# Expert loop of a two-layer backbone: a third staging set for chunks 4, 7 and 10, and loads in the order of the casts

## What is computed

```python
def hier_moe(h, lp):
    lg = (h @ lp['moe_w_group'] + lp['moe_b_group']).astype(jnp.float32)
    ...                                        # top-1 of 4 groups, then top-2 of 4 experts in it
    dense_w = jnp.sum(jax.nn.one_hot(eid, N_EXPERTS, dtype=jnp.float32) * tw[..., None], axis=-2)
    hid = jnp.einsum('bsd,edf->bsef', h, lp['moe_w1'])
    gate, up = jnp.split(hid, 2, axis=-1)
    act = jax.nn.silu(gate) * up * dense_w[..., None].astype(h.dtype)
    return jnp.einsum('bsef,efd->bsd', act, lp['moe_w2'])
```

## Time and profile before

| | us |
|---|---|
| median of 3 runs | 1817.4 (1815.0 to 1821.8) |
| the profiled execution's own time | 1818.3 |
| its span, first to last instruction | 1816.2 |
| PE busy in the span | 1649.1 |
| DVE busy | 1171.0 |
| ACT busy | 891.5 |
| expert loop, first layer | 712.7 to about 893 |
| expert loop, second layer | about 1596 to 1774 |

### The profile page before, as it was taken

The page is one execution under the profiler, slowest core; times in us unless marked ns, Lnnn a source line. Parts: engine busy times, 40 slices in busy tenths (PEclk is TensorE's granted clock), DMA queues, the critical chain, the costliest instruction groups (busy, mean ns, idle before and its releaser), DMA issues.

```text
span 1816.2 us, 34273 instructions
## 1 busy us (share of the span) xinstructions
PE 1649.1 (91%) x13317; PEld 1112.9 (61%) x13317; DVE 1171.0 (64%) x1877; ACT 891.5 (49%) x1477; POOL 491.3 (27%) x434
## 2 busy tenths in 40 slices
PE   5899989999989996988889999899999999799886
PEld 3478766777765555444466886667776655554444
DVE  4495355777636757888556926477774394788874
ACT  3322555666642232777543236466664312358763
POOL 0222253221231311233143315322113321123313
PEclk8999999999999998999979999999999999889998
DMA  9565535532335645999935542232223366489975
GB/s 318 185 210 176 170 133 186 195 112 73 100 122 211 208 142 211 339 378 401 323 146 167 195 160 93 80 103 73 77 77 106 125 235 233 151 299 338 402 291 197
DMA packets 191615, 351.33 MB, mean 193 GB/s; under 512 B 15795, under 2 KB 99314, under 8 KB 191218
## 3 DMA queue, kind: packets, MB, share of 16 engines
q1 hardware_dynamic: 182005, 320.17, 50.2%
q0 software_dynamic: 7776, 28.32, 4.2%
q10 hardware_dynamic: 1693, 0.89, 0.2%
HBM read 288.32 MB, written 61.01 MB: 192 GB/s over the span
## 4 chain that ended last, share of the span: by engine, by line
PE 65%; DVE 11%; DMA 9%; ACT 7%; issue 5%; DVEq 2%; SPq 1%; POOL 1%; ACTq 0%; POOLq 0%
PE PS L444 38%; PE PS L451 11%; PE PS L1179 3%; DMA wf<-in_moe_w 3%; PE PS L1163 3%; DMA arena<-in_moe_w 3%; PE PS L949 2%; DVE arena L2560 2%; PE PS L914 1%; ACT whi L1760 1%; PE PS L931 1%; ACT arena L1591 1%; DMA hpart<-y_rows,wulo 1%; DVE wlo L2560 1%; DVE scratch L2500 1%
## 5 line engine op out<-in xcount | busy, mean ns | idle before, releaser
L1883 POOL TENSOR_TENSOR wlo<-wf,whi 128x256 f16<-128x256 f32 (+1 forms) x276 | 294.8, 1101 | 851.2 <-ACT whi L1507 799.3
L444 PE MATMUL PS<-hpart,whi 128*128 128x320 f16 x2048 | 423.4, 300 | 19.0 <-ACT arena L1591 17.8
L444 PE MATMUL PS<-hpart,wlo 128*128 128x320 f16 x1024 | 306.6, 299 | 0.0
L444 PE MATMUL PS<-whi,hpart 128*128 128x256 f16 (+2 forms) x1536 | 287.8, 288 | 9.9 <-issue 6.3
L444 PEld LDWEIGHTS PS<-hpart,whi 128*128 128x128 f16 x2048 | 190.1, 98 | 108.7 <-issue 39.7
L444 PE MATMUL PS<-wlo,hpart 128*128 128x256 f16 (+2 forms) x768 | 219.5, 288 | 0.0
L444 PEld LDWEIGHTS PS<-whi,hpart 128*128 128x128 f16 x1536 | 148.7, 98 | 66.9 <-issue 29.6
L2366 DVE TENSOR_REDUCE stat<-PS 128x1 f32<-128x640 f32 (+1 forms) x160 | 110.7, 713 | 80.0 <-PE PS L1163 77.5
L451 PE MATMUL PS<-hpart,whi 128*128 128x128 f16 (+1 forms) x768 | 138.8, 304 | 12.4 <-DVE hpart L2041 10.8
L1591 ACT ACTIVATE arena<-PS,pcol 128x320 f32<-128x320 f32 x128 | 67.4, 527 | 168.2 <-PE PS L444 163.1
L2194 DVE SCALAR_TENSOR_TENSOR scratch<-scratch,cw 128x655 f32<-128x655 f32 x120 | 138.6, 1197 | 4.5
(11 more groups left out here) (366 smaller groups left out, 2909.2 us busy)
## 6 DMA issues: line engine op xcount, KB each, us to landing
arena<-in_moe_w SPq DMA_DIRECT2D x68, 1024.0 KB, 8.9
arena<-in_w_ada SPq DMA_DIRECT2D x48, 1024.0 KB, 7.1
wf<-in_w_gate SPq DMA_DIRECT2D x32, 1024.0 KB, 5.7
wf<-in_moe_w SPq DMA_DIRECT2D x32, 1024.0 KB, 8.9
g_rows<-arena SPq DMA_DIRECT2D x128, 160.0 KB, 1.8
wf<-in_w_in SPq DMA_DIRECT2D x18, 1024.0 KB, 9.4
y_rows<-scratch SPq DMA_DIRECT2D x34, 512.0 KB, 8.7
arena<-g_rows SPq DMA_DIRECT2D x24, 640.0 KB, 5.2
```

What stands on the lines that cost most here:

```text
L444: ins = pe.matmul(out, st, mv, start=first and n == 0, stop=last and n == 2)
L1883: ins = pool.tensor_tensor(lo[:, a:b], wf[j][:, a:b], hi[:, a:b], ALU.subtract)
```

## The change

`staged` sends chunks 4, 7 and 10 to set 2, and chunks 5, 6, 8, 9, 11, 12 and so on by turns to sets 0 and 1. So up to chunk 12 a load waits for the low part of the chunk three before it (`c - 3`) instead of two before it; from chunk 13 on it is two again. SP's list of loads is put in the order in which DVE frees the buffers, and chunk 4 is loaded ahead of the rest of chunk 3. On ACT and DVE ten steps are written out instead of four, and on SP too. The counts of `third_in` take the place of `m_once`; two of its three semaphores are shared with `x_in`, which stands for two other loads of the layer. No operation on data is added or removed.

```diff
@@ staged, arrivals
-            return (0, 1, 0, 1, 2)[c] if c < 5 else 1 - c % 2
+            return (0, 1, 0, 1, 2, 0, 1, 2, 0, 1, 2)[c] if c < 11 else 1 - c % 2
-            return (1, 1, 2, 2, 1)[c] if c < 5 else (c + 1) // 2
+            return (1, 1, 2, 2, 1, 3, 3, 2, 4, 4, 3)[c] if c < 11 else (c - 1) // 2
@@ SP: load_early and the list
-                    before = {3: 1, 5: 2, 6: 3}.get(c, c - 2)
+                    before = 1 if c == 3 else c - 3
...
                 sp.wait_ge(*first_in(l, 16))
+                for q in range(3):
+                    load_early(4, q)
                 for q in range(1, 3):
                     load_early(3, q)
-                for q in range(3):
-                    load_early(4, q)
                 load_early(5, 0)
...
-                load_early(5, 1)
-                load_early(6, 0)
                 sp.wait_ge(*filled(0, CHUNKS * 16))
...
-                for c, parts in enumerate((((6, 1), (5, 2)), ((6, 2), (7, 0)), (), ((7, 1), (7, 2), (8, 0)))):
+                for c in range(10):
+                    if c < 8:
+                        load_early(c + 5, 1)
+                        if c:
+                            load_early(c + 4, 2)
+                    elif c == 8:
+                        load_early(12, 2)
+                    else:
+                        load_next(13, 1, 0, 13)
                     store(c, c % 2, P * c)
-                    for part in parts:
-                        load_early(*part)
-                with sp.Fori(3, p + 1) as i:
+                    if c < 7:
+                        load_early(c + 6, 0)
+                    elif c > 7:
+                        load_next(c + 5, 0, c % 2, c + 5)
+                with sp.Fori(5, p) as i:
                     for n in range(2):
-                        store(i * 2 + (n - 2), n, i * (2 * P) + (n - 2) * P)
-                        load_next(i * 2 + (2 + n), 1, 1 - n, i * 2 + (2 + n))
-                        load_next(i * 2 + (2 + n), 2, 1 - n, i * 2 + (2 + n))
-                        load_next(i * 2 + (3 + n), 0, n, i * 2 + (3 + n))
+                        load_next(i * 2 + (4 + n), 1, 1 - n, i * 2 + (4 + n))
+                        load_next(i * 2 + (3 + n), 2, n, i * 2 + (3 + n))
+                        store(i * 2 + n, n, i * (2 * P) + n * P)
+                        load_next(i * 2 + (5 + n), 0, n, i * 2 + (5 + n))
@@ ACT, and DVE in the same way
-                for c in range(4):
+                for c in range(10):
...
-                with act.Fori(2, p + 1) as i:
+                with act.Fori(5, p + 1) as i:
```

More of the change, by code:

```diff
@@ L318, in build @@
         w_lo = sig("w_lo", V_ALL, 1)
-        x_in = [sig(f"x_in{n}", 16) for n in range(2)]
+        x_in = [sig(f"x_in{n}", 4 * 16) for n in range(2)]
         x_hi, x_lo = sig("x_hi", 2), sig("x_lo", 2)
@@ L426, in build @@
         m_in = [sig(f"m_in{n}") for n in range(6)]
-        m_once = sig("m_once", 3 * 16)
+        third_in = [Signal(x_in[0].sem, 4 * 16, 16), Signal(x_in[1].sem, 4 * 16, 16), sig("third_in", 3 * 16)]
         xg_in = [sig(f"xg_in{j}") for j in range(2)]
@@ L778, in load @@
                     sp.dma_start(dst, src.rearrange("o e (k p) n -> p (o e k) n", p=P)
-                                 ).then_inc((m_once if j == 2 else m_in[3 * j + q]).sem, 16)
+                                 ).then_inc((third_in[q] if j == 2 else m_in[3 * j + q]).sem, 16)
                 for j, q in ((0, 0), (0, 1), (0, 2), (1, 2)):
@@ L1754, in part_high @@
                     if slot == 2:
-                        act.wait_ge(*m_once(l, 3 * 16))
+                        act.wait_ge(*third_in[q](l, count * 16))
                     else:
-                        act.wait_ge(m_in[3 * slot + q].sem, ran * 16 + count * 16)
+                        act.wait_ge(m_in[3 * slot + q].sem, ran * 16 + (count * 16 - 16 * l))
                     if not isinstance(c, int) or c >= 2:
@@ L1828, in _ @@
                         act_high(i * 2 + n, n)
-                        part_high(i * 2 + (2 + n), 1, n, 1 - n, i + (1 + n))
-                        part_high(c, 2, j, n, i + 1)
+                        part_high(i * 2 + (2 + n), 1, n, 1 - n, i + n)
+                        part_high(c, 2, j, n, i)
                         rows_high(i * 2 + (2 + n), n)
                         silu(c, j)
-                        part_high(i * 2 + (3 + n), 0, j, n, i + 2)
+                        part_high(i * 2 + (3 + n), 0, j, n, i + 1)
                         rows_back(i * 2 + n, n, i)
                 act_high(p * 2 + 2, 0)
-                part_high(p * 2 + 4, 1, 0, 1, p + 2)
-                part_high(p * 2 + 3, 2, 1, 0, p + 2)
+                part_high(p * 2 + 4, 1, 0, 1, p + 1)
+                part_high(p * 2 + 3, 2, 1, 0, p + 1)
                 rows_high(p * 2 + 4, 0)
@@ L1841, in _ @@
                 act_high(p * 2 + 3, 1)
-                part_high(p * 2 + 4, 2, 0, 1, p + 2)
+                part_high(p * 2 + 4, 2, 0, 1, p + 1)
                 silu(p * 2 + 4, 0)
@@ L2790, in _ @@
                 p = pairs_now(dve)
-                with dve.Fori(2, p + 1) as i:
+                with dve.Fori(5, p + 1) as i:
                     for n in range(2):
```

3 lines of the change are left out of this document (2 added, 1 removed).

## The result

The changed kernel takes 1795.6 us (median of four runs, 1793.0 to 1798.2), the one before 1816.2 beside it (1812.6 to 1821.8). The two medians are 20.6 us apart; the recorded ratio, which is not their quotient (that is 0.989), is 0.987, with a 95% interval from 0.985 to 0.990. By the interval 19 to 27 us of 1817.4 are gone, where 19 were forecast. Two later measurements, on two chips, gave 0.986 and 0.987. The profiled execution took 1793.0 us with a span of 1791.2.

A forecast was written before the change was run, and what follows sets the result against it. The expert loop was taken to begin at PE's pace and end at that of full DMA engines. Winning 10.1 and 8.9 us in the two layers, 19.0 together, gave 1798.4 us from a median of 1817.4; range 1795 to 1808.

The forecast's parts named there:

- The mechanism: Expert loops: casts no longer wait for weight parts, so nine steps per layer run at 9.45 us throughout.
- the quick pace: Early steps of the expert loop, set by PE while weights lie ready: 9.45 us a step.
- the sum: Nine steps at 9.45 us, 85.05 us a layer: 10.1 us won in the first, 8.9 in the second, 19.0 together.
- The lead suffices: Weight loads: bytes leave some 5 us for gaps; a load may take 23.5 us, from chunk 13 on 14.0.
- The steps written out at nothing: Fewer register loads on SP and loop passes on ACT and DVE: taken as 0, between -1 and +1 us a layer.
- (3, 1) hidden: Chunk 3's load behind chunk 4's 3.15 MB, 7.9 us: taken as costing nothing, 2 us a layer kept for the upper end.
- The size: Gain in the expert loops of both layers: 19.0 us, giving 1798.4 us.
- The slow pace: Later loop steps, set by 4.19 MB a step at 399 GB/s: 10.58 us in the first layer, 10.44 in the second.
- What of the change does it: Third set gives more than one step of lead; SP's new order only lets the freed set 2 be refilled.
- The end of the loop at the DMA engines' pace: Rival: a layer's last four steps lose 1.1 us each again, 1806 to 1807 us; chance 0.20, including part of the lead lost.
- Nothing won: Rival: request order limits the 399 GB/s, or casts and low parts hold the steps; time near 1815 us; chance 0.08.
- Slower by the gathers: Rival: row gathers wait behind the deeper weight queue, PE waits 5.5 us every two steps; 1825 us; chance 0.06.

The follow-up runs named there:

- the fillers: Changed kernel with more filler matmuls on PE, into an unread bank, around the expert loops and last combine: 1788.3 us, ratio 0.986; later 1790.0 beside 1793.8 without them.

## Why the prediction was right, and where it missed

*The mechanism.* Right for the waits and the pace. From chunk 6 on the quick pace holds to the end in every profile of the changed kernel: 9.44 us a step against the 9.45 of the sum. The nine steps of the first profile took 84.80 and 84.79 us, against 85.05.

*The lead suffices.* Right, by both of its arguments. The rate in the first stretch rose to 395 GB/s; landing rose to 15 us, fell to 9 and was 12.4 at most towards the end, below the 23.5 and 14.0 us that a load may take.

*The steps written out at nothing, (3, 1) hidden.* Within what can be measured for the first. For the second, ACT waits for no weights between 712 and 780 us.

*The size.* **This is the step that failed.** The slow pace went into the sum as 10.58 and 10.44 us a step, 95.19 and 93.93 us for nine, from one execution. For that execution the subtraction is right: 10.4 + 9.1 = 19.5 us against the 19.0 foreseen. But in five profiles the nine steps of both layers took from 189.1 to 203.1 us, with a mean of 193.9 and a median of 192.4, and the one used was the lowest. After takes 169.6, so the gain of these steps is 24.3 us by the mean and 22.8 by the median instead of 19.0. The total of that profile hid it, since its rest of 1611.0 us was the longest. The runs before, 1815.0 to 1821.8, said that something varied by 7 us. The prediction took that as an offset of 0.9 us to the median and did not ask which steps varied; in the five profiles the slow steps went up from the pace of the first, and eight of them never took less than 83.50 us. Its range started 3 us below its point, too near for a term known from one sample. How far the time itself is off is less sure than the term: the interval of 19 to 27 us begins where the forecast stands.

*What of the change does it.* Partly wrong. The prediction said that three sets give the lead and that the order only lets set 2 be filled. The order gives 16.5 us without a third set, the set 7.2 without the order. The rows for the right answer were there: (7, 1) waited behind two stores until 766.75. With the new order and two sets it leaves by 760.0, with three sets by 752.9.

*The rivals.* The end of the loop at the DMA engines' pace does not occur with three sets; it is what the order alone shows (steps of 10.7 and 11.4 us at the end). Nothing won is refuted. Slower by the gathers was rightly given little. The trace agrees with the Trainium skill (SBUF — State Buffer, "SBUF: two separate sides") as far as POOL's pause before a gather stays (2.4 to 6.7 us, 7.2 at most with the fillers), now that DVE is dense in all steps; whether DVE's hold of the port is its cause was not tried. The "3 to 5 us later" beside that rule was 3.23 less 0.83, 2.4 us, by the rows it cites. The landing of gathers does not grow with SP's queue (8.1 to 8.7 us beside loads of 15), so the two delays do not add, as the sum assumed.

## What to carry to other kernels

Where a loop runs at the pace of full DMA engines, look at the stretch ahead of it: if transfer time is unused there, and loads stand in an in-order list behind a wait that ends later than their own, try the order of that list before another buffer; here it gave more than twice as much. Price such a loop from several executions: here the loop whose casts waited varied by 14 us between profiles, and the version without these waits by less than 0.1 in three. A total that looks like the median can hide a quick loop beside a slow rest.

## What the runs showed of the hardware

- One core moved 404 GB/s over 75 us, loads, stores and gathers together.
- In the eight DMA-limited steps of before the rate was 372 to 402 GB/s in five executions. Most steps took 10.4 us in the first; in the others they took from 9.0 to 14.4.
- PE's granted clock fell to 0.5 for 3.4 us behind a wait of 4.80 us, in the midst of eight steps in which PE is busy for 76.41 of 89.44 us.
- Loads in SP's queue took 15 us to land while gathers in POOL's took 8.1 to 8.7.
- POOL's pause before a gather was 2.4 to 6.7 us in the loops of one execution of the changed kernel, but for the first of each, and 6.9 to 7.2 in the first steps of the one with fillers, whose program for DVE is the same.
